# 512-column operands for u0 and u1 with tile sums on VectorE, no unread identity products, and a layer norm with its gates between conversions

## What is computed

```python
# convolution group of the second block
h = layer_norm(h, conv_ln_g, conv_ln_b)
return silu(h)
# experts
q = (x @ w_q) per head, two halves of 128; scores = q_half @ sub_keys   # 8 heads x 2 halves x 128 keys
top 16 of each half, 16 x 16 sums, top 16 of them; softmax -> gates
out = sum over chosen experts e: gate_e * gelu(x @ u[e]) * v[e]
```

## Time and profile before

| | |
|---|---|
| runs before, us | 3252.38, 3254.93, 3257.09 (median 3254.93) |
| profiled execution, us | 3252.32, of which the span of its instructions is 3250.4 |
| granted TensorE clock, mean | 0.997 |
| busy share of the span | PE 98%, DVE 49%, ACT 46%, POOL 77% |
| u0 in the trace | 1757.2 to 1941.6 us |
| u1 in the trace | 1941.6 to 2136.9 us |
| second attention | about 1493 to 1563 us |
| layer norm of the convolution | about 1575 to 1609 us |

### The profile page before, as it was taken

How to read it: one execution, slowest core, us unless ns; L and a number is a source line. 1 busy time by engine, 2 the same in 40 slices (tenths; PEclk the granted TensorE clock), 3 DMA queues, 4 the chain that set the end, 5 groups by cost and what they waited for, 6 DMA issues and landing times.

```text
span 3250.4 us, 63185 instructions
## 1 busy us (share of the span) xinstructions
PE 3185.0 (98%) x23074; PEld 2848.9 (88%) x23074; DVE 1608.0 (49%) x2967; ACT 1483.1 (46%) x1981; POOL 2497.1 (77%) x1117
## 2 busy tenths in 40 slices
PE   8999889999999999998999999999999999999999
PEld 7888878988888888997789999998888888888888
DVE  3268645522222322496565957676612664157600
ACT  5465544544444445444454553443444334433433
POOL 6821255888888888887587887788898889887887
PEclk9999999999999999999999999999999999999999
DMA  6553203555555555543354555455555555555555
GB/s 224 186 163 127 86 16 130 194 188 188 191 189 188 188 188 186 202 168 106 114 184 169 182 181 174 168 182 175 174 195 187 179 175 186 184 180 174 175 193 168
DMA packets 158764, 553.26 MB, mean 170 GB/s; under 512 B 18000, under 2 KB 24288, under 8 KB 158496
## 3 DMA queue, kind: packets, MB, share of 16 engines
q1 hardware_dynamic: 152208, 541.37, 49.5%
q0 software_dynamic: 3248, 6.77, 0.9%
q10 hardware_dynamic: 3168, 3.15, 0.3%
HBM read 548.33 MB, written 2.88 MB: 170 GB/s over the span
## 4 chain that ended last, share of the span: by engine, by line
PE 81%; DVE 6%; POOL 5%; issue 5%; ACT 2%; DMA 1%; POOLq 0%; ACTq 0%; DVEq 0%; SPq 0%
PE ps L765 39%; PE ps L767 19%; PE ps L753 17%; POOL wl L602 5%; PE ps L1008 2%; DVE wl L1884 1%; PE ps L1325 1%; DVE qhl L1866 1%; DVE from_u L2490 1%; ACT wh L1431 0%; DVE arena L1963 0%; DMA xT<-x 0%; PE ps L832 0%; DMA raw<-w_z 0%; PE ps L1196 0%
## 5 line engine op out<-in xcount | busy, mean ns | idle before, releaser
L602 POOL TENSOR_TENSOR wl<-raw,wh 128x1024 fp32r<-128x1024 f32 x980 | 2364.3, 2421 | 494.2 <-ACT wh L1431 492.0
L1431 ACT ACTIVATE wh<-raw 128x1024 fp32r<-128x1024 f32 (+1 forms) x1034 | 1084.1, 1053 | 1442.1 <-PE ps L767 1111.2
L765 PE MATMUL ps<-uhl,wh 128*128 128x512 f32 x2688 | 940.7, 396 | 11.4 <-DVE uhl L1866 11.3
L767 PE MATMUL ps<-uhl,wl 128*128 128x256 f32 x2688 | 748.5, 278 | 0.0
L753 PE MATMUL ps<-uhl,wh 128*128 128x256 f32 x4000 | 738.0, 287 | 3.2 <-POOL wl L602 1.2
L753 PEld LDWEIGHTS ps<-uhl,wh 128*128 128x128 f32 x4000 | 628.8, 193 | 10.9 <-issue 6.3
L765 PEld LDWEIGHTS ps<-uhl,wh 128*128 128x128 f32 x2688 | 505.9, 188 | 132.1 <-DVE wl L1884 10.1
L753 PE MATMUL ps<-uhl,wl 128*128 128x256 f32 x2000 | 568.1, 284 | 0.0
L765 PE MATMUL ps<-ehl,wh 128*128 128x512 f32 x1536 | 551.5, 400 | 0.0
L767 PEld LDWEIGHTS ps<-uhl,wl 128*128 128x128 f32 x2688 | 507.1, 189 | 0.1
L1875 DVE TENSOR_REDUCE ps<-ps 128x256 f32<-128x512 f32 x168 | 117.5, 699 | 637.2 <-PE ps L767 636.4
(11 more groups left out here) (365 smaller groups left out, 3559.6 us busy)
## 6 DMA issues: line engine op xcount, KB each, us to landing
raw<-w_u SPq DMA_DIRECT2D x256, 512.0 KB, 3.2
raw<-w_v SPq DMA_DIRECT2D x256, 512.0 KB, 3.2
raw<-w_gu SPq DMA_DIRECT2D x176, 512.0 KB, 4.2
raw<-w_down SPq DMA_DIRECT2D x80, 512.0 KB, 3.2
raw<-w_out SPq DMA_DIRECT2D x64, 512.0 KB, 3.2
raw<-w_z SPq DMA_DIRECT2D x54, 512.0 KB, 4.1
raw<-w_in SPq DMA_DIRECT2D x52, 512.0 KB, 3.2
raw<-w_qkv SPq DMA_DIRECT2D x48, 512.0 KB, 3.2
```

What stands on the lines that cost most here:

```text
L602: pool.tensor_tensor(wl[:, slot, 0:width], raw[:, slot, 0:width], wh[:, slot, 0:width].bitcast(F32), ALU.subtract).then_inc(lo_ready, 1)
L765: pe.matmul(bank(b).rearrange("p (n t) -> p n t", n=2), wh[:, slot, at], both, start=first and c == 0, stop=False, skip_group_check=True)
L767: ins = pe.matmul(bank(b)[:, 0:T], wl[:, slot, at], high, start=False, stop=last and c == kt - 1, skip_group_check=True)
L1431: act.activation(wh[:, slot, 0:width], raw[:, slot, 0:width], ACT.Copy).then_inc(hi_ready, 1)
```

## The change

1. `experts_in` uses `pair_unit` for all four quarters. u0 writes banks 4 to 7 in turn, u1 banks 0 and 1. VectorE adds the halves of each tile: for u0 into banks 0 and 1 (`EARLY_SUMS`), amid the routing, at places set by a clock written into the program; for u1 into SBUF (`TILE_SUMS`), between the gate groups and the low parts. The Gelus wait for `exp_sum`. The tiles `topf` and `it16` move from banks 6 and 7 to 2 and 3.
2. `keep_clock` and its calls go.
3. In the layer norm VectorE multiplies before `add_attention2(9)`, and ScalarE does one conversion ahead of the Silus and one behind each four.

```diff
             def experts_in(q, i, k=0, span=1, turn=None, first=False, last=False):
                 for j in range(4):
-                    if first and q == 0 and j < 2:
+                    if first and q == 0:
                         pe.wait_ge(sub_ev, j + 1)
+                    elif q == 0:
+                        pe.wait_ge(exp_sum, i * 4 + (j - 3))
+                    elif first and q == 1 and j < 2:
+                        pe.wait_ge(u_ev, QJ + j - 1)
                     elif first and q >= 2 and j < 2:
                         pe.wait_ge(res_ready, (2 + q) * DT + j - 1)
                     else:
...
+                        pe.wait_ge(exp_sum, i * (4 * span) + (QJ * q + 4 * k + j - 1))
...
-                        if q < 2:
-                            ins = unit(bank(4 * (1 - q) + j % 2)[:, 0:T], ready, g % RING,
-                                       lambda c: uh[:, UKT * n + c, :], lambda c: ul[:, UKT * n + c, :],
-                                       first=n == 0, last=n == 1)
-                        else:
-                            ins = pair_unit(j % 2, ready, g % RING, UHL, UKT * n, first=n == 0, last=n == 1)
+                        ins = pair_unit(4 + j if q == 0 else j % 2, ready, g % RING, UHL, UKT * n, first=n == 0,
+                                        last=n == 1)
...
# TensorE, second attention
-            def keep_clock(b, n):
-                for _ in range(n):
-                    pe.matmul(bank(b)[:, 0:P], ident, ones, start=True, stop=True)
...
-                        keep_clock(LOGIT_BANKS[2 * i % 3], 4 if i in BEFORE_SCORES else 6)
...
-                            keep_clock(3, 2)
...
# ScalarE, layer norm
-            for d in range(LN_VAR_AT, LN_VAR_AT + 2):
-                convert(BASE["out2"] + d + RING)
+            convert(BASE["out2"] + LN_VAR_AT + RING)
             for c in range(WT):
                 act.wait_ge(ln_mul, c // 4 + 1)
...
                 if c % 4 == 3:
                     round_mixed2(c - 3, ln_out, c + 1)
-            for d in range(LN_VAR_AT + 2, DT):
+                    convert(BASE["out2"] + LN_VAR_AT + 1 + c // 4 + RING)
+            for d in range(LN_VAR_AT + 3, DT):
                 convert(BASE["out2"] + d + RING)
...
# ScalarE, gelus
-                    if q < 2:
-                        act.wait_ge(w_used, i * 8 + (g + 2))
+                    act.wait_ge(exp_sum, i * 4 + (QJ * q + j + 1))
+                    if q == 1:
+                        act.activation(HB[q][:, bass.ds(i * 4 + j, 1), :], TILE_SUMS[j % 2].unsqueeze(1),
+                                       ACT.Gelu).then_inc(u_ev, 1)
...
# VectorE, layer norm
-            for d in range(LN_VAR_AT, LN_VAR_AT + 1):
-                add_attention2(d)
             dve.wait_ge(ln_rt, 1)
...
# VectorE, routing
+            TILE_US, TOP_US, PAIR_US, PICK_US, SUM_US = 5.6, 1.5, 3.2, 1.4, 0.75
+            at_us, summed = [2.0], [0]
+            def sum_next():
+                n = summed[0]
+                dve.wait_ge(w_used, BASE["u0"] + 2 * n + 2)
+                if n >= 2:
+                    dve.wait_ge(u_ev, n - 1)
+                else:
+                    dve.wait_ge(sub_ev, 8)
+                add_halves(EARLY_SUMS[n % 2].rearrange("p a t -> p (a t)"), 4 + n % 4).then_inc(exp_sum, 1)
+                summed[0] += 1
+            def sums_between(us):
+                at_us[0] += us
+                while summed[0] < QJ - 2 and at_us[0] >= TILE_US * (summed[0] + 1) + 0.5:
+                    sum_next()
+                    at_us[0] += SUM_US
...
                     top16(SUB[:, t, n, :], top[:, t, n, :], topi[:, t, n, :].bitcast(U32), wk[:, n % 2, 0:NK])
+                    sums_between(TOP_US)
+                if t == 0:
+                    dve.wait_ge(sub_ev, 8)
+                    link(dve.tensor_copy(it16, cst("iota")[:, 0:TOPK]))
...
                     top16(c, val[:, t, h, :], vali[:, t, 0, h, :].bitcast(U32), wk[:, h % 2, :])
+                    sums_between(PAIR_US)
...
+                        sums_between(PICK_US)
...
                     .then_inc(soft_in, 1)
+            while summed[0] < QJ - 2:
+                sum_next()
...
                     .then_inc(route_ready, 1)
+            while summed[0] < QJ:
+                sum_next()
             dve.wait_ge(et_ps, 1)
...
# VectorE, gates of u0 during u1
+            def sum_first(i, k, j, span=1):
+                dve.wait_ge(w_used, i * (8 * span) + (BASE["u1"] + 8 * k + 2 * j + 2))
+                dve.wait_ge(u_ev, i * (4 * span) + (QJ + 4 * k + j - 1))
+                add_halves(TILE_SUMS[j % 2], j % 2).then_inc(exp_sum, 1)
+            def sum_and_gate(i, last=False):
+                for k in range(1, 1 + SPAN):
+                    for at in range(8):
+                        slot = 8 * (k - 1) + at
+                        if at % 2:
+                            sum_first(i, k, at // 2, SPAN)
+                        if slot in (LAST_SLOTS if last else PAIRED_SLOTS):
+                            m = PAIRED_SLOTS.index(slot)
+                            gate(0, i, len(FIRST_SLOTS) + m, PER, more=not last or m < len(LAST_SLOTS) - 1)
+                        elif last and slot > LAST_SLOTS[-1] and at % 2:
+                            low_next()
...
+            def low_next():
+                for k in range(lows_done[0], min(lows_done[0] + 2, 8)):
+                    expert_low(0, k)
+                lows_done[0] += 2
...
+            for j in range(4):
+                sum_first(0, 7, j)
+                low_next()
```

More of the change, by code:

```diff
@@ L431, in build @@
         GATES = [ps[:, 4 + 2 * b:6 + 2 * b, :].rearrange("p n (t k) -> p (n t) k", k=P) for b in range(2)]
-        topf = ps[:, 6, :].rearrange("p (t n k) -> p t n k", t=2, n=2 * PH)
-        it16 = ps[:, 7, 0:TOPK]
+        EARLY_SUMS = [ps[:, b:b + 1, 0:T] for b in range(2)]
+        TILE_SUMS = [misc[:, 896:1152], misc[:, 2176:2432]]
+        topf = ps[:, 2, :].rearrange("p (t n k) -> p t n k", t=2, n=2 * PH)
+        it16 = ps[:, 3, 0:TOPK]
         rstd_ps = ps[:, 2, 0:T]
@@ L1352, in experts_in @@
                     else:
-                        pe.wait_ge(*((u_ev, i * (4 * span) + (QJ * q + 4 * k + j - 1)) if q < 2 else
-                                     (exp_sum, i * (4 * span) + (QJ * (q - 2) + 4 * k + j - 1))))
+                        pe.wait_ge(exp_sum, i * (4 * span) + (QJ * q + 4 * k + j - 1))
                     for n in range(2):
@@ L1373, in experts_out @@
                     elif first and q < NQ - 1:
[L1374 removed]
+                        pe.wait_ge(exp_sum, QJ * (q + 2) + d - 1)
                     else:
@@ L1786, in _ @@
                         .then_inc(sub_ev, 1)
-            def u_bank(q, j):
-                return 4 * (1 - q) + j % 2 if q < 2 else 4 + j
             def gelus(q, i, round_turn=None, rounds={}):
@@ L1798, in gelus @@
                     ahead(g, i, 8)
-                    if q < 2:
-                        act.wait_ge(w_used, i * 8 + (g + 2))
-                    else:
-                        act.wait_ge(exp_sum, i * 4 + (QJ * (q - 2) + j + 1))
-                    act.activation(HB[q][:, bass.ds(i * 4 + j, 1), :], ps[:, u_bank(q, j):u_bank(q, j) + 1, 0:T], ACT.Gelu)\
-                        .then_inc(u_ev, 1)
+                    act.wait_ge(exp_sum, i * 4 + (QJ * q + j + 1))
+                    if q == 1:
+                        act.activation(HB[q][:, bass.ds(i * 4 + j, 1), :], TILE_SUMS[j % 2].unsqueeze(1),
+                                       ACT.Gelu).then_inc(u_ev, 1)
+                    else:
+                        tile = EARLY_SUMS[j % 2] if q == 0 else ps[:, 4 + j:5 + j, 0:T]
+                        act.activation(HB[q][:, bass.ds(i * 4 + j, 1), :], tile, ACT.Gelu).then_inc(u_ev, 1)
             def round_experts(q, k):
@@ L2363, in _ @@
                 dve.tensor_tensor(mix2[:, c:c + 4, :], mix2[:, c:c + 4, :], wide(7), ALU.mult).then_inc(ln_mul, 1)
-            for d in range(LN_VAR_AT + 1, LN_VAR_AT + 4):
+            for d in range(LN_VAR_AT, LN_VAR_AT + 3):
                 add_attention2(d)
             mixed_low2(0)
-            add_attention2(LN_VAR_AT + 4)
+            add_attention2(LN_VAR_AT + 3)
             mixed_low2(4)
-            for d in range(LN_VAR_AT + 5, DT):
+            for d in range(LN_VAR_AT + 4, DT):
                 add_attention2(d)
@@ L2500, in sum_experts @@
                         expert_low(lows_of, 2 * j + 1)
+            def sum_first(i, k, j, span=1):
[13 more added lines that the diff above has]
+                            low_next()
+            lows_done = [0]
+            def low_next():
+                for k in range(lows_done[0], min(lows_done[0] + 2, 8)):
+                    expert_low(0, k)
+                lows_done[0] += 2
             dve.wait_ge(u_ev, QJ)
             one_hots(0, 0, 0)
-            for m in range(len(FIRST_SLOTS)):
-                gate(0, 0, m)
-            with dve.Fori(0, 2) as i:
-                for m in range(PER):
```

(16 more changed lines are left out.)

2 lines of the change are left out of this document (removed).

## The result

The changed kernel takes 3267.8 us (median of 9 runs, 3262.9 to 3273.8), the one before, beside it, 3256.5 us. The ratio is 1.0046, 95% interval 1.0036 to 1.0057: **slower**, by 12 to 19 us by that interval (the medians of all runs differ by 11), and above the range given. The profiled execution took 3265.1 us with a span of 3263.3 us, 12.9 us more than the span before.

What follows compares the result with a forecast made beforehand. TensorE, busy for 98% of the span, was taken as the bound. u0 -0.2, u1 -3.2, v0 +1.5, attention -2.5 and layer norm -1.7 made -6.1 us: 3248.8 us against 3254.9, range 3239 to 3258.

Steps and rivals of the forecast that it cites:

- the signal: In u0, VectorE's go-ahead for ScalarE's exponentials once routing is done; forecast at 1925 to 1927 us in place of 1905.4.
- the u0 sum: Wide products -5.1, TensorE stall +3.4 and late sums +1.5: -0.2 us for u0 (-1.4 to +1.2).
- the second lag: In u0, sums fall behind their tiles because top-16 steps take 1.71 us, not the 1.5 reckoned; priced at 1.5 us.
- The stall: Near u0's end, TensorE waits 3.4 us (3.1 to 4.2) for unit 60, as ScalarE stands before its exponentials.
- u1: Second wide stage: -5.1 from wide products, +1.2 waiting for one-hots, +0.7 for tile 31's bank: -3.2 us.
- v0's first unit: Start of v0: it waits for tile 30's Gelu, whose sum stands behind the last low part; +1.5 us.
- tile 31's bank: End of u1: low parts and sums make VectorE slower than the tiles, so tile 31 waits 0.7 us for its bank.
- Attention: Second attention without identity products: -6.4 us of their time, +3.9 for a lower clock, -2.5 us (-6.4 to +2).
- Layer norm: Earlier conversions on ScalarE remove TensorE's 1.7 us wait for GpSimd's unit 15: -1.7 us.
- The slower one: Rival, 8%: TensorE runs the second attention at 1.2 GHz from the second round to the output blocks; +13, 3268 us.
- Sums late on VectorE: Rival, 20%: pairs at 2.825 us, each sum costing its whole 0.70, low parts at 3.4; -1.9 altogether, 3253.0 us.
- The pace of u2 and u3: Warning sign: these loops' pace differs by 2% for no readable reason, and 3 us either way could come from it.

## Why the prediction was wrong

**The step that failed** is the one that gets the signal by adding the sums' own time to the routing of before: "29 x 0.61 to 0.70 is 17.7 to 20.3 us", and "So the signal comes at 1925 to 1927 in place of 1905.4", which is 168 to 170 us after the start of u0. It took the 149.3 us of routing as fixed, and put the other moves on VectorE at nothing because they "change the order, not the work". The signal came at 189.2. The work itself grew by 22.2 us, since its length of before held only in step with the gaps between splits. The rows showed what was needed: 2.4 us of split per unit, the low parts at 1.21 us alone and 3.42 beside GpSimd, and the rule of the Trainium skill stood in the prediction, but was applied to the low parts and the sums only. What was not asked is why the candidate sum, with two SBUF inputs, took 0.42 us beside an engine that splits for 2.4 of every 2.88 us.

**The rest of the u0 sum held.** With the blocked operations freed, the signal came 167.8 to 168.8 us after the start, a unit took 2.79 to 2.82 us without its waits and the lost clock (2.80 predicted), TensorE waited 2.6 to 2.8 us once near the end (3.4 predicted) and 1.0 to 1.7 once elsewhere (1.5 predicted for the second lag), ScalarE 7.3 for the signal (9 predicted), and u0 lasted 184.3 to 186.1 us (184.2 predicted). The stall went when the exponentials were moved: it was rightly named. In the changed kernel the same chain, 21 us later, made one stall of 7.9 us out of the 3.4, and the second lag, priced at 1.5 us, cost 12.2 us in eight waits of up to 2.8.

A second cost was put at nothing without a reason: what a stall does to the clock of the units behind it. The two windows at the end of u0, changed kernel:

```profile
1930.00:1947.00 17.00, 8.95 (x50) 7.26 (x48) 15.96 (x36) 7.16 (x10) 7.12 (x4) 0.87 0.29 93
1947.00:1961.00 14.00, 13.97 (x64) 12.03 (x65) 0.82 (x2) 5.82 (x8) 13.20 (x6) 0.79 0.63 195
```

After the 7.9 us (1939 to 1947) TensorE works without a pause at a mean clock of 0.79: (1 - 0.79) x 14 = 2.9 us of full-speed work lost. With a mean of 0.98 over the 156 us up to 1910 it is some 6 us, an estimate. 64 x 2.80 + 20.1 + 6 = 205.3 of the 207.4 us.

**u1** was put at -3.2 and v0's first unit at +1.5 us. u1 up to v0's first product is 3.8 us shorter, where the two make -1.7; the waits are 0.6 us for one-hots (1.2 predicted), none for tile 31's bank (0.7 predicted), and 0.2 and 0.4 for splits at v0's start where 1.5 was put. The direction held; the low parts behind the sums cost less.

**Attention** was put at -2.5 us: the medians of the kernel before with and without the products say -3.3, and its traces, from the first head to u0, 261.9 against 257.0 us. The clock fell as foreseen, in more and longer stretches. If the products' own 6.4 us are right, it cost 1.5 to 3.1 us and not the 3.9 put on it; why it cost less isn't shown. **Layer norm** was put at -1.7: TensorE's one wait of 1.7 us is gone in every kernel with the new order, and nothing stands in its place. From the last head's copy to u0 the two kernels with the new order and the products take 203.6 us, and the three with the old one 205.6. The medians say -3.7, with an interval that holds both.

**The rivals.** The slower one named 3268 us, and 3267.8 was measured; that is luck, for its mechanism was the clock in attention, and attention got shorter. "Sums late on VectorE" was nearest in kind, but counted only their own time. The pace of u2 and u3 changed, as the prediction warned: u3 gave some 2.8 us back, hiding part of the loss in the profiled pair.

Open is why the part of the change outside u0 (11.7 to 13.7 us below before, by its ratios) is a little more than its parts measured alone (3.3, 3.7 and 3.8 us in u1): the intervals allow it.

## What to carry to other kernels

Before something is inserted into a queue beside a GpSimd that reads SBUF nearly all the time, list the VectorE instructions with no end in PSUM (two SBUF inputs; copies, casts and tensor-scalar operations from SBUF to SBUF) and price each at a whole GpSimd instruction: that they are short in the trace may only mean that two periods happen to match. The cheapest mend is an end in PSUM: either one for an operation with one input, and one of the operands for one with two (a result in PSUM alone was not tried there). And where three engines stand in a ring, as here with Gelu, conversion and split, a sum that comes late can be paid for twice, once as a stall and once in the clock behind it.

## What the runs showed of the hardware

- The same instruction, 256 results from two SBUF operands: 0.42 us in a gap of GpSimd, 2.62 us against it (median of 16 in one kernel), 0.42 us always with one operand in PSUM. MAX8, FIND_INDEX8 and MATCH_REPLACE8 on SBUF kept their 0.27 to 0.43 us beside the splits, and a reduction from SBUF to SBUF (256 elements to 16 results) its 0.42, in every kernel looked at.
- The clock behind a stall is not settled by its length: after 2.6 us it fell (0.78 over the next 14 us), after 2.8 us in the kernel next to it not at all.
- A loop's pace is not a property of its code. The same kernel, profiled twice, had tiles of 5.55 us in u3 in one execution (the first two rows) and of 5.66 in the other:

```profile
2824.78 0.70 DVE L1874 TENSOR_REDUCE ps<-ps 128x256 f32<-128x512 f32 x1 [4.86 <-PE ps L769]
2830.32 0.70 DVE L1874 TENSOR_REDUCE ps<-ps 128x256 f32<-128x512 f32 x1 [4.84 <-PE ps L769]
```

```profile
2819.88 0.70 DVE L1874 TENSOR_REDUCE ps<-ps 128x256 f32<-128x512 f32 x1 [4.95 <-PE ps L769]
2825.54 0.70 DVE L1874 TENSOR_REDUCE ps<-ps 128x256 f32<-128x512 f32 x1 [4.96 <-PE ps L769]
```

  Of the 14 traces, ten have one of u2 and u3 at the longer pace, and all behind u1 then takes 1111.9 to 1113.8 us; four have neither, and 1110.8 to 1111.1. The wide u1 took 191.0 to 191.4 or 193.3 to 193.5 us, but no kernel profiled twice shows both. In the wide u0 the pace changed where TensorE had stalled: with the exponentials one Gelu later from 5.55 to 5.65 us behind the stall of 1.7 us, and with the index operations' results in PSUM from 5.65 to 5.55 behind its first, of 1.0 us. The spans of that kernel's two profiles are 3238.3 and 3245.4 us: 4.8 us lie ahead of the second attention and 2.7 behind u1, with nothing in the code to explain them. So a change worth 3 us has to be read from medians.
